# The opening of a decoder layer: two weight tiles as plain fp32 products, and sums of squares on other engines

## The reference, cut to what matters

```python
def rmsnorm(x, g):
    x32 = x.astype(jnp.float32)
    inv = lax.rsqrt(jnp.mean(x32 * x32, axis=-1, keepdims=True) + RMS_EPS)
    return (x32 * inv * g.astype(jnp.float32)).astype(x.dtype)

def in_projection(x, norm_g, w_in):
    h = rmsnorm(x, norm_g) @ w_in
    return jnp.split(h, [int(c) for c in np.cumsum(IN_SPLITS)[:-1]], axis=-1)
...
    mem_kv = (rmsnorm(mem, mem_norm_g) @ w_mem_kv).reshape(b, mem.shape[1], 2, MEM_HEADS, HEAD_DIM)
```

## Time and profile before

| | us |
|---|---|
| median of 3 runs | 1194.43 (1193.56 to 1195.64) |
| the profiled execution, device time | 1194.23 |
| its span in the trace | 1192.4 |
| PE busy | 1146.2 (96%) |
| DVE busy | 607.0 (51%) |
| ACT busy | 390.9 (33%) |
| POOL busy | 128.8 (11%) |

### The profile page before, as it was taken

How to read it: one execution, slowest core, us unless ns; L and a number is a source line. 1 busy time by engine, 2 the same in 40 slices (tenths; PEclk the granted TensorE clock), 3 DMA queues, 4 the chain that set the end, 5 groups by cost and what they waited for, 6 DMA issues and landing times.

```text
span 1192.4 us, 19820 instructions
## 1 busy us (share of the span) xinstructions
PE 1146.2 (96%) x8210; PEld 1098.2 (92%) x8210; DVE 607.0 (51%) x873; ACT 390.9 (33%) x533; POOL 128.8 (11%) x177
## 2 busy tenths in 40 slices
PE   4998999999999999999999999999999999999993
PEld 3998999998899999998999999999999999999993
DVE  7384444422326576565555547544554554544444
ACT  4253232211234444443323234333333333332330
POOL 7964000000000000000000000000000000002221
PEclk8898999999999999999999999999999999999997
DMA  6565576533454332246686853344444444464432
GB/s 229 187 229 198 194 248 238 176 115 141 158 181 136 119 107 77 103 145 221 230 294 228 284 167 138 142 141 152 164 144 142 147 159 153 142 229 157 160 106 88
DMA packets 62583, 201.79 MB, mean 169 GB/s; under 512 B 6112, under 2 KB 36400, under 8 KB 44016
## 3 DMA queue, kind: packets, MB, share of 16 engines
q1 hardware_dynamic: 57776, 185.35, 45.4%
q0 software_dynamic: 2288, 10.94, 2.7%
q10 hardware_dynamic: 2448, 4.48, 1.0%
HBM read 193.53 MB, written 11.41 MB: 172 GB/s over the span
## 4 chain that ended last, share of the span: by engine, by line
PE 90%; DVE 5%; DMA 2%; ACT 1%; issue 1%; POOL 0%; ACTq 0%; DVEq 0%; SPq 0%; POOLq 0%
PE bank L991 26%; PE bank L993 26%; PE bank L992 26%; PE bank L1069 3%; DMA raw<-in_stream 2%; DVE w_lo L644 1%; DVE h_lo L669 1%; PE bank L1129 1%; PE bank L1108 1%; PE bank L1163 1%; DVE m_lo L669 1%; DVE y_out L974 1%; PE bank L1089 1%; DMA x_t<-in_x_t 1%; ACT w_hi L459 1%
## 5 line engine op out<-in xcount | busy, mean ns | idle before, releaser
L991 PE MATMUL bank<-h_hi,w_hi 128*128 128x320 f32 x1584 | 497.1, 314 | 4.4 <-DVE w_lo L644 3.7
L992 PE MATMUL bank<-h_lo,w_hi 128*128 128x320 f32 x1584 | 490.6, 310 | 0.0
L993 PE MATMUL bank<-h_hi,w_lo 128*128 128x320 f32 x1584 | 490.5, 310 | 0.0
L459 ACT ACTIVATE w_hi<-raw 128x2048 fp32r<-128x2048 f32 x139 | 266.2, 1915 | 669.2 <-PE bank L993 610.4
L644 DVE TENSOR_TENSOR w_lo<-raw,w_hi 128x2048 fp32r<-128x2048 f32 x139 | 325.0, 2338 | 176.7 <-ACT w_hi L459 176.7
L991 PEld LDWEIGHTS bank<-h_hi,w_hi 128*128 128x128 f32 x1584 | 298.5, 188 | 10.6 <-DVE w_lo L644 5.3
L992 PEld LDWEIGHTS bank<-h_lo,w_hi 128*128 128x128 f32 x1584 | 298.6, 189 | 0.5
L993 PEld LDWEIGHTS bank<-h_hi,w_lo 128*128 128x128 f32 x1584 | 298.3, 188 | 0.0
L991 PE MATMUL bank<-oz_hi,w_hi 128*128 128x320 f32 x256 | 79.8, 312 | 1.8 <-issue 1.8
L993 PE MATMUL bank<-oz_hi,w_lo 128*128 128x320 f32 x256 | 79.7, 311 | 0.0
L992 PE MATMUL bank<-oz_lo,w_hi 128*128 128x320 f32 x256 | 79.6, 311 | 0.0
(11 more groups left out here) (273 smaller groups left out, 1127.4 us busy)
## 6 DMA issues: line engine op xcount, KB each, us to landing
raw<-in_stream SPq DMA_DIRECT2D x143, 1024.0 KB, 5.0
cmp_t<-in_cmp_pages SPq DMA_DIRECT2D x32, 128.0 KB, 4.2
kt_moba<-in_moba_k SPq DMA_DIRECT2D x16, 256.0 KB, 5.4
kt_mem<-in_mem_k SPq DMA_DIRECT2D x8, 512.0 KB, 6.3
vs_moba<-in_moba_v SPq DMA_DIRECT2D x16, 256.0 KB
vs_mem<-in_mem_v SPq DMA_DIRECT2D x8, 512.0 KB
x_t<-in_x_t ACTq DMA_DIRECT2D x4, 640.0 KB, 9.9
y_t<-in_x_t POOLq DMA_DIRECT2D x1, 2560.0 KB, 9.8
```

What stands on the lines that cost most here:

```text
L459: nc.scalar.activation(w_hi[:, u], raw[:, u], ACT.Copy).then_inc(hi_ready[u], 1)
L991: nc.tensor.matmul(out[:, 0:n], w_hi[:, u, kb, :], hi[:, kb, :], start=(kb == first), stop=False)
L992: nc.tensor.matmul(out[:, 0:n], w_hi[:, u, kb, :], lo[:, kb, :], start=False, stop=False)
L993: mm = nc.tensor.matmul(out[:, 0:n], w_lo[:, u, kb, :], hi[:, kb, :], start=False, stop=(kb == last))
```

## The change

Four things are done together.

1. Tiles (0,0) and (1,0) are no longer split. DVE multiplies the raw weights by the gains in place (`gained`; the gain belongs to the row of the weight as much as to x), and PE multiplies them as plain fp32 with the raw `x_t`: 16 matmuls for a tile instead of 48. `raw[u]` is then free only when PE is done, so SP waits for `mm_done` before it loads the next tile there.
2. The squares move to ACT, whole groups of four blocks at a time (`x_sq`, `m_sq`), and POOL adds them up in five larger operations each (`sum_blocks`). `m_sq` lies where `x_t` was.
3. The work after that is in another order on every engine: on PE the sum over x before the tile (1,1), the sum over the memory and the folding of the gates before (0,3) instead of after (1,3); on ACT the squares of the memory between `w_hi` of (1,1) and (0,2); on DVE three of the inverse roots' neighbours, shown below.
4. `gains` is loaded by SP, the second weight tile only when the third quarter of x is there, and the memory rows all together behind tile (0,1).

```diff
             sp.sem_inc(raw_ready[0], 16)
+            sp.dma_start(gains[:], A["gains"]).then_inc(gains_in, 16)
...
+            sp.wait_ge(x_in[2], 16)
             weight_tile(1, 0)
             for u in range(2):
+                sp.wait_ge(mm_done[u], 2)
                 weight_tile(u, 1)
-                memory_rows(2 * u)
-                memory_rows(2 * u + 1)
+                if u == 0:
+                    for n in range(4):
+                        memory_rows(n)
...
+            def sum_blocks(sq, total, squared, summed):
+                for n in range(1, 4):
+                    pool.wait_ge(squared, n + 1)
+                    nc.gpsimd.tensor_tensor(sq[:, 0:4], sq[:, 0:4], sq[:, 4 * n:4 * n + 4], ALU.add).then_inc(summed, 1)
+                    pool.wait_ge(summed, n)
+                nc.gpsimd.tensor_tensor(sq[:, 0:2], sq[:, 0:2], sq[:, 2:4], ALU.add).then_inc(summed, 1)
+                pool.wait_ge(summed, 4)
+                nc.gpsimd.tensor_tensor(total, sq[:, 0, :], sq[:, 1, :], ALU.add).then_inc(summed, 1)
...
+            for n in range(4):
+                nc.scalar.activation(x_sq[:, 4 * n:4 * n + 4], x_t[:, 4 * n:4 * n + 4], ACT.Square).then_inc(x_squared, 1)
             for u in range(2):
                 split_hi(u, 1)
-            for u in range(2):
-                split_hi(u, 2)
+            act.wait_ge(lo_x, KB)
+            act.wait_ge(gn_done, 1)
+            act.wait_ge(x_squared, 4)
+            for n in range(4):
+                act.wait_ge(m_in[n], 16)
+                nc.scalar.activation(m_sq[:, 4 * n:4 * n + 4], m_t[:, 4 * n:4 * n + 4], ACT.Square).then_inc(m_squared, 1)
+            split_hi(0, 2)
             act.wait_ge(rms_v, 1)
             nc.scalar.activation(inv[:], rt[:, 0, :], ACT.Sqrt).then_inc(rms_r, 1)
+            split_hi(1, 2)
...
+            def gained(w, kbs, width):
+                g = gains[:, 0, kbs].unsqueeze(2).to_broadcast([P, kbs.stop - kbs.start, width])
+                return nc.vector.tensor_tensor(w, w, g, ALU.mult)
...
+                pe.wait_ge(x_in[kb // 4], 16)
+                pe.wait_ge(wg0_rdy, kb // 4 + 1)
+                mm = nc.tensor.matmul(W[0][:, 0:TOK], raw[:, 0, kb, :], x_t[:, kb, :], start=(kb == 0), stop=(kb == KB - 1))
             mm.then_inc(mm_done[0], 1)
-            part(1, 0, h_hi, h_lo, TOK, ALL)
...
+            pe.wait_ge(wg1_rdy, 1)
+            for kb in range(KB):
+                mm = nc.tensor.matmul(W[1][:, 0:TOK], raw[:, 1, kb, :], x_t[:, kb, :], start=(kb == 0), stop=(kb == KB - 1))
+            mm.then_inc(mm_done[1], 1)
+            pe.wait_ge(lo_x, KB)
             part(0, 1, h_hi, h_lo, TOK, ALL, S0, spare=True)
```

## The result

| | before | after |
|---|---|---|
| median (4 runs each), us | 1194.8 (1193.56 to 1195.64) | 1201.1 (1200.43 to 1203.92) |
| span of the profiled execution, us | 1192.4 | 1201.8 |
| tile (1,0) done, "T1", us | | 44.5 (forecast 30.6) |
| start of the memory tiles, us | 87.8, effectively 95.0 | 101.3 |

The ratio is 1.0056, with a 95% interval from 1.0043 to 1.007: the changed kernel is 6.3 us slower. The forecast was 7 us faster, range 1181 to 1194. The profiled execution is the slowest of the four of after (1203.9, 2.8 over the median), so its span says a little too much. The start of the memory tiles, 101.3 against 95.0, gives the 6.3 us of the medians; that the two agree to a tenth is luck, since behind that start this execution took 3.4 us longer than the profiled one of before for the same code.

A forecast was written before the change was run, and what follows sets the result against it. PE bounds the kernel, busy 96% of the span. Effective memory-tile start 95.0 less the new 86.8 or 89.9 gains 8.2 or 5.1 on 1194.2: 1186.0 or 1189.1, forecast 1187; range 1181 to 1194, without rivals 1 and 2.

The forecast's parts named there:

- effectively 95.0: Undisturbed memory-tile start giving before's same end: 87.78 plus 4.9 us PE idle and 2.3 for the low clock.
- Part 1: Opening up to the end of plain tiles (0,0) and (1,0): PE no longer waits for DVE, T1 = 30.6.
- Part 2: From T1 to the memory tiles: a load meeting the copy delays PE; effective start T1 + 56.2 or T1 + 59.3.
- the start 9.1 instead of 7.5: First plain matmul of (0,0), claimed near 7.5 us because x's first quarter now leads its queue.
- The new stall before (1,1): PE waits 2 us since SP loads (1,1) only at T1; up to 4.3 with clock drop, swallowed by a later wait.
- copy ahead: Copy `win_old` issued before the load of (1,3), which it slows: memory tiles effectively at T1 + 59.3, 1189.1 us, chance 0.32.
- Rival 2: Clock stays low in the plain tiles (0,0) and (1,0): T1 = 47.5, everything behind 16.9 later, 1204 us; chance 0.07.
- Rival 1: At the copy `win_old`: a load beside it takes at most 10.2 us, effective start 80.8, 1180 us; chance 0.10.
- the first case: Load of (1,3) issued before the copy, load of (0,4) hit: memory tiles effectively at T1 + 56.2, 1186.0 us; chance 0.35.
- Rival 3: POOL's long adds cost more than their columns: copy issued at T1 + 31, 1191 to 1194 us; chance 0.12.

The follow-up runs named there:

- the kernel with the sums later: The changed kernel with one wait added: POOL begins its sums over x only when DVE has gained the weights of tile (1,0); 1189.84 us, ratio to before 0.9954.

## Why the prediction was wrong, point by point

**The step that failed** is in Part 1: "tile (1,0) 8.8 (its weights are loaded by about 17, and gained in 2.3)". The load landed at 18.4, about when DVE was free for it, and the gains by themselves took 2.3 where POOL was held back. What is missing is what stands ahead of the gains on DVE, the last low part of x: the forecast put it at nothing, and it took 11.13 us. I had DVE's durations "with POOL quiet" there, and never asked what POOL does at that time. It isn't quiet: ACT's squares start at 15.2 and POOL's adds at 17.7, just before DVE comes to the last quarter of x at 18.6. The rule that I used in Part 2 for the memory's adds (an operation of the one waits for a whole operation of the other), and even named as speaking against the change, I did not apply to x's adds, some twenty microseconds earlier. Put in, it would have given: one group of four, three of them waiting for an add. The prediction's own 2.2 ns a column makes 2.8 us of 1280 columns, so 1.9 + 3 x 2.8 = 10.3 (measured 11.1: the adds took 3.0, and the fourth operation waited too, for the add of 640 columns). From 18.6 on that ends at 28.9, and the gains at about 31.2; (1,0), cold, takes 11.9, as the forecast's (0,0) did: T1 = 43.1, 12.5 later than written, and a time of nearly 1200. The length of the adds, the cold start and h_hi's end (18.8) stood in rows of before; the 1.9 did not, since in before DVE never made a group without company.

The 13.9 us by which T1 missed, term by term: the start 9.1 instead of 7.5, of which 0.3 came back in (0,0) and the gates, makes 1.3; the wait 9.55, in which the gains' 2.9 instead of 2.3 is contained; the low clock in (1,0) 3.1. The start was late since x's first quarter, put first in its queue, was there at 5.1, but the first weights landed only at 8.2 (5.3 in before): of two loads that are both needed one had come forward and the other gone back, and I moved only the first.

**Part 2 held in the main**, measured from T1. The new stall before (1,1) is 1.76 us (2 forecast); the copy is issued at T1 + 24.6 (26.2); the load that meets it lands at T1 + 42.6 (45.6 forecast) and is that of (1,3), the case "copy ahead"; PE starts (1,3) after 6.4 us of idling, at T1 + 47.4, and the memory tiles at T1 + 56.7. The case that came true had 59.3; the difference is the load, which landed 3.0 sooner, since the copy was issued 1.6 sooner and took 16.5 instead of 17.7. So a part of the closeness is luck: T1's 13.9 us on the 1189.1 of that case would be 1203.0, and 1201.1 was measured. POOL's adds of 1024 columns took 2.41, 2.62 and 4.34 us (forecast 2.42), the last one beside DVE's `w_lo`.

**The chance and the range.** None of the rivals was this one. Rival 2 (the low clock in the plain tiles, 1204) has the number nearly right and the cause wrong: (0,0) took 11.7 us (forecast 11.9), slow at its beginning only, and (1,0) was slow for its first 6 us, after PE had stood for 9.55. In the kernel with the sums later, (1,0) ran at full speed in 8.88. The granted clock alone would not have shown (0,0)'s slow beginning: in after it reads 1.00 until 25 us, while the matmuls take 741 ns up to about 14 us and 432 behind. Rival 1 (the copy slows nothing decisive) was wrong here, and its price of 10.2 us for a load beside the copy was what pieces of 4 KB then gave (8.6 to 10.9). Its sum has a slip: the load's end at +43 and the same 8.3 us behind it as in the first case make +51.3, not +50.2, so 1181. Rival 3 had the adds of the memory in mind only.

**By the pages.** The lock that the Trainium skill's page "SBUF — State Buffer" (SBUF: two separate sides) states for a DVE operation with two SBUF inputs against a reading GpSimd agrees with these traces, to the operation: 1.93, 4.37 and 11.13 us for the same four operations beside nothing, 320-column and 1280-column adds. The Trainium skill's page "DMA: Bandwidth & Descriptors" (Queues, rings and completion order) says that a DMA engine goes round between queues a packet at a time. The packet counts agree: 32 to 32 beside long rows, 164 to 181 beside short ones. I had taken the 14.28 us of before as evidence against the rule, and that was the error: equal turns by packet are equal shares of the bytes only where the packets are equally long, and the copy's were eight times the load's.

## What to carry to other kernels

When a change makes the operations of one engine fewer and longer, go through the orders of the engines that share something with it, and ask for each operation that overlaps them in time what stands behind it in its queue; a rule found in one place of the kernel is to be applied in all. A slow operation costs nothing where the next one in its queue isn't waited for, so moving the waited-for one ahead, or the long ones behind it, cures the same loss (11.3 and 11.6 us here for one line each). And a big background copy should not be issued in pieces much longer than those of a load that is waited for beside it (64 KB against 8 KB here); with short pieces it lands later itself, which matters where something waits for it.

## What the runs showed of the hardware that I had not expected

- A short DVE operation beside long POOL ones isn't slowed by a factor, it waits for a whole one each time: a 0.544 us operation took up to 3.195 us beside adds of 3.02, 1.815 beside one of 1.66, up to 1.152 beside adds of 0.86 to 1.01. The two engines take turns, so the price is about the number of the one's operations times the length of the other's.
- Two DMA queues share the engines packet for packet, whatever the packets' lengths: 32 of 64 KB to 32 of 8 KB, 181 of 4 KB to 164 of 8 KB. A load of 1 MB took 16.8 us beside pieces of 64 KB, 8.6 to 10.9 beside pieces of 4 KB, mostly 4.8 to 5.3 alone. The copy landed 25 to 26 us after its first issue instead of 16.2.
- PE at the high clock from its first real matmul is to be had by giving it idle products beforehand: 28 recorded matmuls of 128 columns, from 1.7 us on (433 ns instead of 741 in the first real ones). Here it brought nothing, since DVE was next.
- The granted clock of the profile can read 1.00 ahead of its first change (25 us in after) while matmuls take 741 ns instead of 432; the matmuls' own lengths are the safer sign there.
